# Prompt stick-breaking attention as products of sigmoids, two heads at a time

## The reference, cut to what matters

```python
def stick_breaking_attention(q, k, v, bias):
    for qs in range(0, Lq, blk):                      # blk = 128
        ke = off + qs + blk                           # off = 0 for the prompt
        z = einsum("bqhd,bkhd->bhqk", q[:, qs:qs + blk], k[:, :ke]) / sqrt(d) + bias_f
        causal = arange(ke)[None, :] < qpos[:, None]  # strictly before the query
        log_1mb = where(causal, log_sigmoid(-z), 0.0)
        later = cumsum(log_1mb, axis=3, reverse=True) - log_1mb
        w = where(causal, exp(log_sigmoid(z) + later), 0.0)
        outs.append(einsum("bhqk,bkhd->bqhd", w, v[:, :ke]))
```

## Time and profile before

| | |
|---|---|
| median of three runs | 4465.39 us |
| the profiled execution | 4464.68 us, span 4462.9 us |
| mean granted TensorE clock over the span | 0.913 |
| the stage `stick_prompt` | about 242.8 to 553.9 us of the span |
| busy in 243 to 554: PE, DVE, ACT, POOL | 247.1, 281.5, 173.8, 134.6 us |

### The profile page before, as it was taken

One profiled execution on the slowest core, in us unless ns is written; L12 is line 12 of the kernel. 1 busy time (PEld: TensorE's weight loads), 2 busy tenths in 40 slices (PEclk: granted clock), 3 DMA queues, 4 the chain that ended last, 5 costly groups with the idle time before them and its releaser, 6 DMA issues. The chain is left out here.

```text
span 4462.9 us, 65960 instructions
## 1 busy us (share of the span) xinstructions
PE 3913.9 (88%) x25477; PEld 3086.8 (69%) x25477; DVE 2095.7 (47%) x3360; ACT 1191.4 (27%) x2372; POOL 642.2 (14%) x608
## 2 busy tenths in 40 slices
PE   7988788888868999999998798667998789999997
PEld 7955456666654488898885466335777459889986
DVE  2179966666685434433432422434106453443345
ACT  2145555555541121111113212211012112111112
POOL 0034411111100111111110010025100111111112
PEclk9977799999989999999999898678885889999999
DMA  2210099999903011111101100036500301111111
GB/s 88 69 43 1 7 374 407 405 405 404 381 10 108 1 48 38 46 47 38 47 29 71 36 31 27 8 110 239 182 20 13 125 29 38 38 47 47 38 47 59
DMA packets 215766, 468.53 MB, mean 105 GB/s; under 512 B 31241, under 2 KB 124277, under 8 KB 212422
## 3 DMA queue, kind: packets, MB, share of 16 engines
q1 hardware_dynamic: 208246, 457.94, 28.0%
q10 hardware_dynamic: 7280, 7.34, 0.5%
HBM read 445.34 MB, written 19.89 MB: 104 GB/s over the span
## 5 line engine op out<-in xcount | busy, mean ns | idle before, releaser
L1810 DVE TENSOR_TENSOR x<-x,f_d 128x512 f32<-128x512 f32 (+1 forms) x576 | 391.4, 686 | 326.2 <-PE f_d L1671 323.0
L1671 PE MATMUL f_u<-xH,f_w1h 128*128 128x364 f32 (+1 forms) x1536 | 508.4, 331 | 23.3 <-DVE f_w1l L1802 23.3
L1671 PE MATMUL f_u<-xL,f_w1h 128*128 128x364 f32 (+1 forms) x1536 | 508.1, 331 | 0.0
L1671 PE MATMUL f_u<-xH,f_w1l 128*128 128x364 f32 (+1 forms) x1536 | 507.8, 331 | 0.0
L1671 PE MATMUL f_d<-f_w2h,f_hh 128*128 128x512 f32 x1152 | 458.3, 398 | 14.4 <-DVE f_w2l L1802 8.8
L1671 PE MATMUL f_d<-f_w2l,f_hh 128*128 128x512 f32 x1152 | 457.0, 397 | 0.0
L1671 PE MATMUL f_d<-f_w2h,f_hl 128*128 128x512 f32 x1152 | 456.8, 397 | 0.0
L1784 POOL TENSOR_TENSOR f_hl<-f_h,f_hh 128x364 fp32r<-128x364 f32 (+1 forms) x192 | 184.6, 968 | 1331.9 <-ACT f_hh L1750 1331.9
L1826 DVE TENSOR_TENSOR f_h<-f_h 128x364 f32<-128x364 f32 (+1 forms) x192 | 103.0, 537 | 557.6 <-ACT f_h L1744 557.6
L1671 PEld LDWEIGHTS f_u<-xH,f_w1h 128*128 128x128 f32 x1536 | 291.7, 190 | 25.4 <-issue 24.2
L1671 PEld LDWEIGHTS f_u<-xL,f_w1h 128*128 128x128 f32 x1536 | 291.6, 190 | 1.3
(11 more groups left out here) (487 smaller groups left out, 6703.9 us busy)
## 6 DMA issues: line engine op xcount, KB each, us to landing
ss_kv<-in_cache_sb_kv SPq DMA_DIRECT2D x336, 512.0 KB, 8.3
x<-in_cache_sb_kv SPq DMA_DIRECT2D x176, 512.0 KB, 8.4
w<-in_ffn_w SPq DMA_DIRECT2D x64, 1024.0 KB, 5.2
mp_qb<-mp_q SPq DMA_DIRECT2D x24, 1024.0 KB, 7.1
x<-in_x_prompt SPq DMA_DIRECT2D x16, 512.0 KB, 8.9
pe_raw<-in_w_in_even SPq DMA_DIRECT2D x8, 1024.0 KB, 6.0
mp_kc<-in_cache_dil_kv SPq DMA_DIRECT2D x8, 1024.0 KB, 7.3
mp_vc<-in_cache_dil_kv SPq DMA_DIRECT2D x8, 1024.0 KB, 5.0
```

Of the source, the lines that this page charges most:

```text
L1671: mm = pe.matmul(out, a, b, start=(n == 0), stop=(n == len(parts) - 1))
L1810: v.tensor_tensor(K.x[0:r, t, cs], K.x[0:r, t, cs], dn_b[(c * DOWN + u) % 4][0:r, :], ALU.add).then_inc(added, 1)
```

## The change

The unit of work becomes a step: a pair of heads (0 and 1, 2 and 3, ...) and one query block. There are 32 steps, with the sizes in the same order. Unit 2s is the even head of step s, unit 2s+1 the odd one.

- PE puts the scores of the even head in `zp[0]` and of the odd head in `zp[1]`, alternating between the two, and then adds the mask of -1e30 on the last 128 keys by a matmul with the identity. Scores of a step wait until ACT has finished all four reads of the previous one.
- ACT reads the scores twice: sigmoid of minus z into `l`, sigmoid of z into `z`.
- DVE runs one scan, a running product of `l` from the last key down to key 1. It no longer reads scores, takes a maximum or multiplies a mask.
- POOL multiplies `z` by `l` shifted by one key. The result is the weights; `w` and the third activation are gone, and so is POOL's mask.
- `wT` is copied by ACT for even units and by DVE for odd ones. The output copy takes both heads at once, 128 rows.
- PE's order in step s is: transpositions of unit 2(s-2), scores of step s, values of step s-3 with the heads alternating, transpositions of unit 2(s-2)+1. DVE's is: output of step s-4, scan 2s, copy of unit 2(s-2)+1, scan 2s+1. ACT's is: copy of unit 2(s-2), then the four sigmoids of step s.
- There are eight `z` buffers (four of them in the part of `K.xT` that is idle here), six `l`, four `wT`.

The new code, with a few of the removed lines:

```diff
-    units = [(h, qb) for h in range(SBH) for qb in [*range(0, SEQ // P, 2), *reversed(range(1, SEQ // P, 2))]]
...
+    NB = SEQ // P
+    steps = [(c, qb) for c in range(SBH // 2) for qb in [*range(0, NB, 2), *reversed(range(1, NB, 2))]]
+    NSP = len(steps)
+    ZS, LS, TS = 8, 6, 4
     with ExitStack() as ctx:
         sb = lambda name, shape: ctx.enter_context(nc.sbuf_tensor("sp_" + name, shape, F32))
-        z, l = (sb(n, [P, 3, SEQ]) for n in ("z", "l"))
-        w, wT = (sb(n, [P, 2, SEQ]) for n in ("w", "wT"))
-        masks, bias, cap, ones = sb("masks", [P, 2, P]), sb("bias", [P, SBH]), sb("cap", [P, SBH]), sb("ones", [P, 1])
+        zs, l, wT = sb("z", [P, ZS - 4, SEQ]), sb("l", [P, LS, SEQ]), sb("wT", [P, TS, SEQ])
+        z = [zs[:, i] for i in range(ZS - 4)] + [K.xT[:, 4 + i, 0:SEQ] for i in range(4)]
+        hide, bias, less, none = sb("hide", [P, P]), sb("bias", [P, SBH]), sb("less", [P, SBH]), sb("none", [P, 1])
         zp = [ctx.enter_context(nc.psum_tensor(f"sp_zp{i}", [P, SEQ], F32)) for i in range(2)]
         tp = ctx.enter_context(nc.psum_tensor("sp_tp", [P, SEQ], F32))
         op = [ctx.enter_context(nc.psum_tensor(f"sp_op{i}", [P, 512], F32)) for i in range(2)]
...
+        loaded, cleared, logits, left, share, summed, weights, turned, out_done, out_copied, kept = (
+            K.sem("sp_" + n) for n in ("ld", "clr", "lg", "left", "share", "sum", "w", "trn", "od", "oc", "kept"))
+        wT_ready = [K.sem("sp_wTa"), K.sem("sp_wTv")]
+        keys = lambda u: (steps[u // 2][1] + 1) * P
         with nc.Block() as block:
             @block.sync
             def _(sp):
-                sp.dma_start(masks[:, 0, :], io["c_strict"]).then_inc(loaded, 16)
-                sp.dma_start(masks[:, 1, :], io["c_strict_neg"]).then_inc(loaded, 16)
+                sp.dma_start(hide[:, :], io["c_strict_neg"]).then_inc(loaded, 16)
                 sp.dma_start(bias[:, :], io["sb_bias"][0].partition_broadcast(P)).then_inc(loaded, 16)
                 I.load(sp)
                 space.load(sp)
...
 
             @block.tensor
             def _(pe):
...
+                def scores(p):
+                    c, qb = steps[p]
+                    ke = (qb + 1) * P
+                    if p >= 1:
+                        pe.wait_ge(share, 2 * p)
                     for n in range(0, ke, 512):
                         m = min(512, ke - n)
...
+                        for hh in range(2):
+                            lo = HD * hh
+                            pe.matmul(zp[hh][:, n:n + m], T["qT"][lo:lo + HD, c, qb * P:(qb + 1) * P],
+                                      T["kT"][lo:lo + HD, c, n:n + m], start=True, stop=(n + m < ke))
+                    if p == 0:
+                        pe.wait_ge(loaded, 32)
+                    for hh in range(2):
+                        mm = pe.matmul(zp[hh][:, ke - P:ke], K.ident[:, :], hide[:, :], start=False, stop=True)
                     mm.then_inc(logits, 1)
 
                 def turn_weights(u):
                     pe.wait_ge(weights, u + 1)
                     if u >= 1:
...
+                        pe.wait_ge(wT_ready[(u - 1) % 2], (u - 1) // 2 + 1)
+                    for kb in range(keys(u) // P):
+                        mm = pe.transpose(tp[:, kb * P:(kb + 1) * P], z[u % ZS][:, kb * P:(kb + 1) * P], K.ident[:, :])
                     mm.then_inc(turned, 1)
 
...
+                def values(p):
+                    c, qb = steps[p]
+                    for hh in range(2):
+                        pe.wait_ge(wT_ready[hh], p + 1)
+                    if p >= 2:
+                        pe.wait_ge(out_copied, p - 1)
                     for kb in range(qb + 1):
...
+                        for hh in range(2):
+                            lo, h = HD * hh, 2 * c + hh
+                            mm = pe.matmul(op[p % 2][lo:lo + HD, 0:P], T["v"][:, kb, h * HD:(h + 1) * HD],
+                                           wT[:, (2 * p + hh) % TS, kb * P:(kb + 1) * P], start=(kb == 0), stop=(kb == qb))
                     mm.then_inc(out_done, 1)
 
...
+                for s in range(NSP + 3):
+                    if 0 <= s - 2 < NSP:
+                        turn_weights(2 * (s - 2))
+                    if s < NSP:
                         scores(s)
...
+                    if 0 <= s - 3:
+                        values(s - 3)
+                    if 0 <= s - 2 < NSP:
+                        turn_weights(2 * (s - 2) + 1)
 
             @block.vector
             def _(v):
...
+                v.memset(none[:, :], 0.0).then_inc(cleared, 1)
                 I.clear(v)
...
-                step(v.tensor_scalar(cap[:, :], bias[:, :], -HD ** 0.5, ZCAP * HD ** 0.5, ALU.mult, ALU.add))
...
+                v.wait_ge(cleared, 1)
+                v.wait_ge(loaded, 32)
+                v.tensor_scalar(less[:, :], bias[:, :], -1.0, None, ALU.mult).then_inc(cleared, 1)
                 v.tensor_copy(T["qTs"][:, :, :], T["qT"][:, :, SEQ:NT]).then_inc(kept, 1)
                 v.tensor_copy(T["kTs"][:, :, :], T["kT"][:, :, SEQ:NT]).then_inc(kept, 1)
                 v.tensor_copy(T["vs"][:, :], T["v"][0:NSMP, TT - 1, :]).then_inc(kept, 1)
 
...
+                def left_before(u):
+                    ke = keys(u)
+                    v.wait_ge(left, u + 1)
+                    v.tensor_tensor_scan(l[:, u % LS, 1:ke][:, ::-1], l[:, u % LS, 1:ke][:, ::-1],
+                                         none[:, 0:1].to_broadcast([P, ke - 1]), 1.0, ALU.mult, ALU.add).then_inc(summed, 1)
+                def copy_weights(u):
+                    v.wait_ge(turned, u + 1)
+                    if u >= TS:
+                        v.wait_ge(out_done, (u - TS) // 2 + 1)
+                    v.tensor_copy(wT[:, u % TS, 0:keys(u)], tp[:, 0:keys(u)]).then_inc(wT_ready[1], 1)
+                def keep_output(p):
+                    c, qb = steps[p]
+                    v.wait_ge(out_done, p + 1)
+                    v.tensor_copy(K.xT[:, c, qb * P:(qb + 1) * P], op[p % 2][:, 0:P]).then_inc(out_copied, 1)
+                for s in range(NSP + 4):
                     if 0 <= s - 4:
                         keep_output(s - 4)
+                    if s < NSP:
+                        left_before(2 * s)
+                    if 0 <= s - 2 < NSP:
+                        copy_weights(2 * (s - 2) + 1)
+                    if s < NSP:
+                        left_before(2 * s + 1)
 
             @block.gpsimd
             def _(g):
...
+                for u in range(2 * NSP):
+                    ke = keys(u)
+                    g.wait_ge(share, u + 1)
                     g.wait_ge(summed, u + 1)
...
+                    g.tensor_tensor(z[u % ZS][:, 0:ke - 1], z[u % ZS][:, 0:ke - 1], l[:, u % LS, 1:ke], ALU.mult).then_inc(weights, 1)
 
             @block.scalar
             def _(a):
...
+                def shares(u):
+                    h, ke = 2 * steps[u // 2][0] + u % 2, keys(u)
+                    a.wait_ge(logits, u // 2 + 1)
+                    if u >= LS:
+                        a.wait_ge(weights, u - LS + 1)
+                    a.activation(l[:, u % LS, 0:ke], zp[u % 2][:, 0:ke], ACT.Sigmoid, bias=less[:, h:h + 1], scale=-HD ** -0.5).then_inc(left, 1)
+                    if u >= ZS:
+                        a.wait_ge(turned, u - ZS + 1)
+                    a.activation(z[u % ZS][:, 0:ke], zp[u % 2][:, 0:ke], ACT.Sigmoid, bias=bias[:, h:h + 1], scale=HD ** -0.5).then_inc(share, 1)
+                def copy_weights(u):
+                    a.wait_ge(turned, u + 1)
+                    if u >= TS:
+                        a.wait_ge(out_done, (u - TS) // 2 + 1)
+                    a.activation(wT[:, u % TS, 0:keys(u)], tp[:, 0:keys(u)], ACT.Copy).then_inc(wT_ready[0], 1)
+                a.wait_ge(loaded, 32)
+                a.wait_ge(cleared, 2)
+                for s in range(NSP + 2):
+                    if 0 <= s - 2:
+                        copy_weights(2 * (s - 2))
+                    if s < NSP:
+                        shares(2 * s)
+                        shares(2 * s + 1)
 
 
 STEPS = NPAGES // 2
```

More of the change, by code:

```diff
@@ L507, in sum_later @@
-                def sum_later(u):
-                    ke = (units[u][1] + 1) * P
-                    v.wait_ge(log1p, u + 1)
-                    lu = l[:, u % 3, 0:ke]
-                    step(v.tensor_tensor(lu, z[:, u % 3, 0:ke], lu, ALU.max))
-                    step(v.tensor_tensor(l[:, u % 3, ke - P:ke], l[:, u % 3, ke - P:ke], masks[:, 0, :], ALU.mult))
-                    v.tensor_tensor_scan(l[:, u % 3, 0:ke][:, ::-1], ones[:, 0:1].to_broadcast([P, ke]),
-                                         l[:, u % 3, 0:ke][:, ::-1], 0.0, ALU.mult, ALU.add).then_inc(summed, 1)
@@ L527, in _ @@
+                for s in range(NSP + 4):
                     if 0 <= s - 4:
                         keep_output(s - 4)
+                    if s < NSP:
[4 more added lines that the diff above has]
+                        left_before(2 * s + 1)
```

(33 more changed lines are left out.)

53 lines of the change are left out of this document (removed).

## The result

The changed kernel takes 4371.45 us (median of four runs, 4361.81 to 4376.54) against 4465.53 (4463.4 to 4469.92) for the kernel before beside it. The ratio is 0.9788, 95% interval [0.9776, 0.9799]. 4370 was forecast. The profiled execution took 4367.9 us, its span is 4365.7.

The account below looks back on a forecast made before the run. DVE's instruction list was taken to bound the stage. Steps of 208 us (between 183 and 233 by clock) plus 8 at the ends make 216 for 311 us, 95 less: 4464.7 - 95 = 4370 us, range 4335 to 4412.

Parts of the forecast that it names:

- I take the middle: Stage's PE clock: half the time at each level, so 208 us between 183 at 2.4 GHz and 233 at 1.2.
- Loop A: DVE scans and POOL products exclude each other at the SBUF port: mean 5.52 us a step, 177 us in all.
- rival 2: The port is not held against the scan, so Loop C alone leads: 4365 us; chance 0.10.
- Loop C: Queue round through scores, mask, sigmoid, scan, DVE's copy, transpositions: mean 5.4 us a step at 2.4 GHz, 7.3 at 1.2.
- rival 3: PE stays at 1.2 GHz; its chain of scores, values, transpositions and DVE's copy takes 7.97 us a step: 4417 us; chance 0.09.
- The mask: Two full matmuls on PE after each step's scores, four records of 0.107: 0.43 us, 0.85 at the slow clock.
- The heads side by side: On PE two heads' alternating scores and values run together; scores cost 1.67 us per 1000 keys for both at 2.4 GHz.
- The ends: Time outside the steps: 4.5 us ahead of the stage's first scan and about 3.5 us behind its last product.
- rival 5: Every ACT change between Copy and Sigmoid loads a table, two loads or 2.6 us a step: 4414 us; chance 0.02.
- The other stages: Stages outside the changed one stay as long; one changing by more than 2 us would show the forecast wrong.
- DVE idle while POOL and ACT are idle too: Sign in the changed stage's profile that would show the forecast wrong; no size given.
- loops A to C: Three pace-setting loops of a step: SBUF port, score banks (scores alternating with sigmoids, mean 4.6 us at 2.4 GHz), queues.

Follow-up runs that it names:

- the reordering: Changed kernel with PE running the odd unit's transpositions ahead of the values of step s-3; 4355.09 us, ratio 0.9759.
- the second comparison: The changed kernel measured again without any edit, against the kernel before; 4372.49 us, ratio 0.9807.
- the two best orders: Changed kernel, odd transpositions ahead of values, DVE's copy ahead of both scans; scan's zero in SBUF 4322.56 us, in PSUM 4328.54 and 4324.43 us.

## Why the prediction was right, and what in it was not

The total came out within 2 us. The bound that was removed and the size of the gain were right; the pace of single steps was wrong in both directions, and that the sum came out so near is luck.

- **What was the bound.** DVE's list was: taking it away freed the stage, and the run with single heads shows that the new arithmetic gives the whole gain without pairing (with six `z` and four `l` buffers in place of three each).
- **The steps.** Forecast: 183 us for 32 steps at the fast clock, and half of the 50 us that the slow one would add, 208. Measured: the smallest periods above sum to 47.46, four times 190; the 31 periods of the profiled execution sum to 209.0, with 5.43 for the last step to 214.4 (212.7 from the first scan's start to the last one's end). So 190 + 24 where I had 183 + 25.
- **The clock.** The step "I take the middle" failed: the mean is 0.86 and not 0.75, about 28% of the time at 1.2 GHz (reckoned from the mean). The cost still was 24 us, as the slow stretches fell on the large steps: a step of 896 keys took 8.7 to 9.8 us in three of four cases for 7.10 at best.
- **Loop A, the port.** The hold is as the rule and the earlier trace rows had it (the zero in PSUM removes it). The step that failed is taking it as the pace from 640 keys on: a step of 1024 keys took 7.21 us at best where A gave 9.29. The loop through scan and DVE's copy sets it at least in part: with copy and scan out of that loop, steps of 896, 1024 and 768 keys took 6.67, 6.90 and 5.38 us for 7.10, 7.21 and 6.41. Taking the hold away altogether leaves the steps as long as they were at the fast clock (640 keys could not be compared), and the total within a microsecond. As rival 2 it would have given the same total, 4365, so the total could not tell the two apart; the experiments did: the hold exists, and it sets no pace.
- **Sizes combined per step, each with its own size.** This is the main step that failed. Loop C was summed as if a 256-key step turned and copied 256 keys: 3.4 us. The links belong to steps one to three back, up to 1024 keys, and it took 5.43. For the same reason rival 3's chain was set aside as one for the slow clock. It paces the small steps at the fast clock, as the reordering shows: with the values put behind it, steps of 128, 512 and 256 keys lost 1.06, 0.68 and 1.33 us. With four steps of 512 and 256 keys and three of 128 (the first is not paced by it) that is 11 us, of the 17.4 between the medians. In the large steps the lag helps, since the links of small units stand in them. Per set of eight sizes, 128, 256, 384 and 512 keys took 5.9 us more than forecast, 640 to 1024 keys 4.3 less; four times the difference, 6.4 us, is what 190 has over the forecast's 183.
- **The mask.** Priced at 0.43 us, measured at 0.64 from start to start, and 0.59 to 0.71 in five of the sizes: a term of 14 us that was really some 20. The scores in front of it show the same: 0.64 us from start to start for 0.43 at 256 keys.
- **The product.** Priced at 1.40 us on average from the earlier trace rows, 1.2 measured. Off the path, so without effect.
- **The heads side by side.** Right, for values as well: the forecast took a pair at the price of a single head, and 32 records of two heads take 1.97 us where the earlier trace rows has 1.96 for the 16 of one. It was not worth what it saves PE, since PE's values are on the path in the small steps only. Undoing it in part costs 14 us of stage and 8.5 us between the medians.
- **The ends.** The first scan started 6.0 us into the stage and the last one ended 6.4 us before its end, 12.4 for 8. The table load does stand behind ACT's wait for the first scores, and it is the only one in the stage, so rival 5 is out:

```profile
246.19 1.28 ACT L548 ACT_TABLE_LOAD   x1 [4.58 <-PE sp_zp L460]
```

- **The other stages.** They were to stay within 2 us, and this sign of a wrong forecast came: the first stretch of `dilated_prompt` took 59.7 us for 63.4. That is not scatter. From PE's first to its last matmul there it takes 59.3 to 59.9 us in each of the twelve profiled executions of kernels with paired heads, and 63.0 in the kernel before and in the run with single heads. DVE waits there for a mask, whose transfer (from issue to landing, last number) takes 3.9 us before and 2.1 after:

```profile
dq_mask<-c_bandmask SPq DMA_DIRECT2D x1, 128.0 KB, 3.9
...
dq_mask<-c_bandmask SPq DMA_DIRECT2D x1, 128.0 KB, 2.1
```

The first instruction behind that wait starts 3.9 us into the stretch in the kernel before, 4.2 with single heads, and 2.0 to 2.2 in the twelve. Why the mask lands sooner no run shows. So some 4 of the 11.5 us came with the pairing by a way that the forecast does not have, and they are as much as the 4.1 us between the medians of the run with single heads and of the change. The rest is within the scatter: spans less the stage range over 4141 to 4151 us in the kernels with paired heads, with 4141 for the execution at hand, 4152 before and 4157 with single heads. By the medians the change is worth 94 us, and 91 in the second comparison.
- **DVE idle while POOL and ACT are idle too.** This sign came as well: from 297.74 to 298.46 in the timeline above only PE works. It is the chain through values and odd transpositions, which loops A to C leave out.

## What to carry to other kernels

When stages of a pipeline work on different units of different sizes, write each loop's sum with the size that each link really has in that step; a sum per step with one size misses the chain that paces half of them. After an engine has been relieved, look for a ring of in-order queues (here PE, DVE and back) and move the instruction that others wait for ahead of those for which nobody waits: two such moves gave 1.1% where taking PE from 219 to 161 busy us had given nothing. A resource that is really contended is worth only what the ring leaves no slack for, so price it by taking it away, not by its sum.

## What the runs showed of the hardware

- A scan with both operands in SBUF is held by a POOL product under way (3.03 us on average at 1023 keys, 3.65 at most), and a product by a scan under way (2.91 for 2.00 us). With one of the scan's operands in PSUM neither is (2.27 to 2.28 and 2.00 us).
- POOL's instruction with two operands takes 2357 ns at 1024 elements and 1996 at 1023 with one operand shifted by one; multiplication or subtraction makes no difference.
- Matmuls of two heads on different halves of PE's columns run side by side: 32 records in 1.97 us, against 3.33 one head after the other.
- A pair of full matmuls between matmuls of the halves costs 0.64 us for 0.43 us of columns; leaving it out made five of eight sizes 0.59 to 0.71 us shorter.
- With PE busy for 191.5 of 192.5 us the mean clock was 1.00; in the changed kernel, with PE busy for 161 of 225 us, it was 0.86, and 0.92 to 0.94 in the three executions of the two best orders.
